# The two down projections read their tokens in another order

## The chip, the cores and the metric

The kernel runs on one core of one Trainium2 chip. The metric is the device time of one execution in microseconds (us). TensorE multiplies, VectorE (DVE), ScalarE (ACT) and GpSimd (POOL) work on the elements beside it, and the SP queue issues the loads of the weights. On-chip operands lie in SBUF, sums of TensorE in the eight banks ps0 to ps7 of PSUM.

## The reference, cut to what matters

256 tokens of width 2048 pass two transformer blocks. Each block ends with a feed-forward part, whose last product is the down projection and a residual sum:

```
x = x + (silu(h @ w_gate) * (h @ w_up)) @ w_down            # block 1, hidden width 5632
h = h + (silu(conv(gate)) * conv(val)) @ w_down_2           # block 2, hidden width 5632
```

The sum over the hidden width is made for each token by itself: the order in which the tokens are gone through changes nothing in the result, as long as each sum is added to its own token.

## The kernel before, in words

Everything is held transposed: features on the 128 partitions, the 256 tokens (T) along the free dimension. X is the residual stream, 16 tiles of 128 features x 256 tokens in float32. HID holds the hidden activations of a feed-forward part: 44 tiles (FT) of 128 features x 256 tokens, each in two parts, a high part rounded to the reduced format fp32r and a low part with what is left.

The weights pass through as "units". A unit is 2048 columns: two row tiles of 128 x 1024, brought by the SP queue with two loads of 512 KB into one of four slots of RAW. ACT writes its rounded copy to HIW (line 606, two slots), DVE writes the difference to LOW (line 1073, in the slot of RAW), and TensorE uses both. For each of the unit's two row tiles and each of eight blocks of 128 output columns, `unit` issues three matmuls, high weight times high activation (L1947), high times low (L1948) and low times high (L1949). So a unit is 2 x 8 x 3 = 48 matmuls. The stationary operand is the 128 x 128 block of weights; the moving operand is the activation tile, 256 columns of 4 bytes that lie one behind the other; the output goes to columns 0 to 255 of bank f. A large part of the program (input, output, gate and up projections) does this with H_ROWS as the moving operand; the down projections do it with HID.

A down projection (`down` in each engine's program) is two halves of 1024 output features. Each half is 22 units over the 44 tiles of HID and sums into the eight banks; then `residual` on DVE (L1650) adds the eight banks to eight tiles of X, one instruction of 128 x 256 for each bank, and frees the bank with `bank_freed`. TensorE's first matmul into a bank of the next half waits for that. The first down projection is followed by the projections of the attention, the second by 32 transposes of X (L2454), copies to OUTT and the stores of the output.

The order between engines is kept by semaphores alone: ACT waits until TensorE is through with the unit two before (`unit_used`), DVE for ACT (`hi_made`), TensorE for DVE (`lo_made`).

Of the kernel before, what the change touches and what calls it, by code (L numbers as in the profile page):

```python
# [20 lines left out]
ALU = mybir.AluOpType  # L21
# [4 lines left out]
T = 256  # L26
# [59 lines left out]
def build(nc, io, out):  # L86
    with ExitStack() as ctx:
# [6 lines left out]
        def S(name):  # L94
            if name in after:
                name = after[name][0]
            if name not in sems:
                sems[name] = ctx.enter_context(nc.semaphore(name))
            return sems[name]
# [21 lines left out]
        def at(name, shape, offset, dt=F32):  # L121
            return nc.alloc_sbuf_tensor_at(name, shape, dt, offset=offset)
# [10 lines left out]
        X = at("X", [P, KT, T], o); o += 16384  # L133
# [111 lines left out]
        HID = at("HID", [P, 2, FT, T], r2, F32R)  # L245
# [31 lines left out]
        ps = [ctx.enter_context(nc.psum_tensor(f"ps{i}", [P, 512], F32)) for i in range(8)]  # L277
# [10 lines left out]
        U_DOWN1 = U_FFN1 + 11 * UG  # L288
# [4 lines left out]
        U_DOWN2 = U_FFN2 + 11 * UG  # L293
# [5 lines left out]
        N_DOWN1 = N_FFN1 + 88  # L299
# [3 lines left out]
        N_DOWN2 = N_FFN2 + 88  # L303
# [3 lines left out]
        M_IN, M_OUT, M_FFN1, M_DOWN1, M_FOX, M_OUT2, M_FFN2, M_DOWN2 = 2, 44, 58, 135, 149, 191, 205, 282  # L307
# [4 lines left out]
        bank_freed = S("bank_freed")  # L312
# [747 lines left out]
        def _(dve):  # L1060
            V = nc.vector
# [7 lines left out]
            def lo(u_const, g=None, stepu=0):  # L1069
                v = u_const + 1  # L1070
                dve.wait_ge(hi_made, v if g is None else g * stepu + v)
                n = unit_cols(u_const)
                V.tensor_tensor(LOW[:, u_const % 4, 0:n], RAW[:, u_const % 4, 0:n],  # L1073
                                HIW[:, u_const % 2, 0:n].bitcast(F32), ALU.subtract).then_inc(lo_made, 1)

            def summed(n7, f, u_end, g=None, nf=8, stepu=UG):
                if f < nf - 1:
                    v = n7 + f + 1
                    dve.wait_ge(tile_summed, v if g is None else g * 7 + v)
                else:  # L1080
                    v = u_end + FREE_UNITS
                    dve.wait_ge(unit_used, v if g is None else g * stepu + v)
# [24 lines left out]
            def h_low(k, fs):  # L1107

                c = COL[GAIN[k]]
                for f in fs:  # L1110
                    dve.wait_ge(S("h_hi"), KT * k + f + 1)
                    V.scalar_tensor_tensor(H(1, f, f + 1)[:, 0, :], X[:, f, :], vec[:, c + f:c + f + 1],  # L1112
                                           H(0, f, f + 1)[:, 0, :].bitcast(F32), ALU.mult, ALU.subtract)\
                        .then_inc(S("h_made"), 1)
# [18 lines left out]
            for i, pack in list(enumerate(PACKS))[1:]:  # L1133
                r = sum(n for _, n in pack)
                b = 3 + (i - 1) % 5
# [507 lines left out]
            o_low(3).then_inc(S("mix_made"), 1)  # L1643


            def residual(m0, u_end, half):
                for f in range(GROUP):
                    summed(m0, f, u_end)
                    x = X[:, half * 8 + f, :]
                    V.tensor_tensor(x, x, ps[f][:, 0:T], ALU.add).then_inc(bank_freed, 1)  # L1650

            def out_phase(u0, m0, k):
                for j in range(2, UG + 1):
                    lo(u0 + j)
                residual(m0, u0 + UG, 0)
                lo(u0 + UG + 1)
                u = u0 + UG
                for j in range(2, UG + 1):
                    lo(u + j)
                    if j < 6:  # L1660
                        h_low(k, (2 * j - 4, 2 * j - 3))
                residual(m0 + 7, u + UG, 1)
                lo(u + UG + 1)
                h_low(k, range(8, KT))

            def down(u0, m0, last=False):
                b = u0
                with dve.Fori(0, 4) as i:
                    for j in range(4):
                        lo(b + 6 + j, i, 4)  # L1670
                lo(b + 22)
                residual(m0, b + 22, 0)
                lo(b + 23)
                b = u0 + FT // 2
                for j in range(4):
                    if not last and j < 2:
                        h_low(2, range(4 * j, 4 * j + 4))
                    lo(b + 2 + j)
                with dve.Fori(0, 4) as i:
                    for j in range(4):  # L1680
                        lo(b + 6 + j, i, 4)
                if not last:
                    lo(b + 22)
                residual(m0 + 7, b + 22, 1)
                if not last:
                    lo(b + 23)
                    h_low(2, range(8, KT))
# [5 lines left out]
            def ffn_phase(u0, evac, tail, k, eps):  # L1693
                for j in range(2, UG):
                    lo(u0 + j)
                    if j == 6:
                        variance(k, eps)
                    elif j == 7:
                        inverse_root(k)
                with dve.Fori(0, 10) as g:  # L1700
                    lo(u0 + UG, g, UG)
                    evac(g)
                    for j in range(1, UG):
                        lo(u0 + UG + j, g, UG)
                        tail(g, j)
                lo(u0 + 11 * UG)
                evac(10)
                for j in range(1, UG):
                    if j < 6:
                        lo(u0 + 11 * UG + j)  # L1710
                    tail(10, j)
# [14 lines left out]
                                    HID[:, 0, bass.ds(g * 4, 4), :].bitcast(F32), ALU.subtract)\  # L1726
                        .then_inc(S("hid_made"), 1)
            ffn_phase(U_FFN1, evac_ffn1, tail_ffn1, 1, 1e-5)
            down(U_DOWN1, M_DOWN1)

            def evac_fox(g):
                for f in range(GROUP):
# [167 lines left out]
                                    HID[:, 0, bass.ds(g * 4, 4), :].bitcast(F32), ALU.subtract)\  # L1900
                        .then_inc(S("hid_made"), 1)
            ffn_phase(U_FFN2, evac_ffn2, tail_ffn2, 3, 1e-6)
            down(U_DOWN2, M_DOWN2, last=True)
            for q in range(4):
                got("turned_v")
                V.tensor_copy(OUTT[:, 1, q * 512:(q + 1) * 512], ps[4 + q][:, :]).then_inc(S("y_tokens_1"), 1)
# [3 lines left out]
        def _(pe):  # L1910
# [50 lines left out]
            def group_phase(u0, n0, groups, wcol=plain, h_wait={}):  # L1961
                with pe.Fori(0, groups) as g:
                    for j in range(UG):
                        unit(u0 + j, [2 * j, 2 * j + 1], GROUP, wcol, j == 0, j == UG - 1, g, UG, n0, h_wait=h_wait.get(j))
# [13 lines left out]
                    if j == 4:  # L1978
                        square_sums_out(k, pairs)

            def down(u0, n0, made0):

                for half in range(2):
                    b = u0 + half * (FT // 2)
                    for j in range(2):
                        unit(b + j, [2 * j, 2 * j + 1], GROUP, plain, j == 0, n0=n0 + 8 * half,
                             hcol=lambda part, k: HID[:, part, k, :], h_wait=(S("hid_made"), made0 + 10))
                    with pe.Fori(0, 4) as i:
                        for j in range(4):
                            unit(b + 2 + j, [4 + 2 * j, 5 + 2 * j], GROUP, plain, g=i, step=4,  # L1990
                                 hcol=lambda part, k: HID[:, part, bass.ds(i * 8 + k, 1), :])
                    for j in range(18, 22):
                        unit(b + j, [2 * j, 2 * j + 1], GROUP, plain, last=j == 21,
                             hcol=lambda part, k: HID[:, part, k, :], h_wait=(S("hid_made"), made0 + 11))

            pe.sem_inc(unit_used, FREE_UNITS)
            pe.wait_ge(S("ident_made"), 1)
            for n in range(NT):
# [5 lines left out]
                for q in range(4):  # L2004
                    for i in range(4):
                        f = 4 * q + i
# [4 lines left out]
            for j in range(4):  # L2011
                if j == 3:
                    pe.wait_ge(S("vecs_landed"), counts["vecs_landed"])
                    for i, pack in list(enumerate(PACKS))[1:]:
                        r = sum(n for _, n in pack)
                        b = 3 + (i - 1) % 5
                        if i <= 5 and b > 3:
                            pe.wait_ge(S("x_second"), b - 3)
                        if i > 5:
                            pe.wait_ge(S("vecs_made"), i - 4)  # L2020
                        nc.tensor.transpose(ps[b][:, (i // 6) * P:(i // 6) * P + r], VPACK[0:r, i, :],
                                            ident[0:r, 0:r]).then_inc(S("vecs_turned"), 1)
                unit(j, [4 * j + i for i in range(4)], 3, lambda kk, f: kk * 384 + f * P, j == 0, j == 3,
                     n0=N_MISC1, h_wait=0)
# [89 lines left out]
            for fill, kind in enumerate(FILLS):  # L2114
# [4 lines left out]
                dst, i = ps[fill % 8], place[kind]  # L2119
# [58 lines left out]
            for c in range(NCH):  # L2178
                cc = slice(c * C, c * C + C)
                s0 = ST[:, c % 2]  # L2180
                for hb in range(2):
                    if c:
                        got("s_out")
                    for i in range(4):
                        t = 4 * hb + i
# [17 lines left out]
                for hb in range(2):  # L2203
# [3 lines left out]
                    for i in range(4):  # L2207
                        t = 4 * hb + i
# [4 lines left out]
                for hb in range(2):  # L2213
# [3 lines left out]
                    for i in range(4):  # L2217
                        t = 4 * hb + i
# [29 lines left out]
            for lev in range(1, 6):  # L2248
# [15 lines left out]
                for c in range(NCH):  # L2264
                    got("inv_pm")
                    b = INV_BANKS[c]
# [98 lines left out]
            group_phase(U_OUT, N_OUT, 2, h_wait={0: (S("mix_made"), 1), 4: (S("mix_made"), 2)})  # L2365
            first_group(U_FFN1, N_FFN1, 1, ((SUM_BANK, NSQ[:, 0, :]),), gate_up_col)
            group_phase(U_FFN1 + UG, N_FFN1 + 8, 10, gate_up_col)
            down(U_DOWN1, N_DOWN1, 1)

            def sum_squares(g):  # L2370
                pe.wait_ge(S("sq_lo"), g)
# [73 lines left out]
            group_phase(U_OUT2, N_OUT2, 2)  # L2445
            first_group(U_FFN2, N_FFN2, 3, ((SUM_BANK, NSQ[:, 0, :]),), gate_up_col)
            group_phase(U_FFN2 + UG, N_FFN2 + 8, 10, gate_up_col)
            down(U_DOWN2, N_DOWN2, 12)

            pe.wait_ge(bank_freed, N_END + FREE_BANKS)  # L2450
            for n in range(NT):
# [21 lines left out]
```

## Time and profile before

| what | value |
|---|---|
| median of 3 runs | 2509.73 us (2506.45 to 2510.35) |
| profiled execution, its own time | 2507.64 us |
| its span | 2505.9 us |
| TensorE busy | 2439.3 us, 97% of the span |
| DVE / ACT / POOL busy | 1484.8 / 1122.4 / 114.1 us |
| mean granted clock of TensorE | 0.992 of full speed |
| read from HBM | 427.59 MB |

The span is what the profile covers; the execution's own time is 1.74 us longer. Matmuls are pipelined: the durations of single ones overlap, so their pace is read from the distance between starts, not from the durations.

### The profile page before, as it was taken

To read this page: it belongs to the slowest core of one execution; us is meant where nothing else is said; L and a number is where in the kernel's file an instruction comes from. 1 tells how busy PE (TensorE), PEld (TensorE's weight loads), DVE (VectorE), ACT (ScalarE), POOL (GpSimd) and SP (SyncE) were. 2 spreads that over 40 slices of the span, in tenths; PEclk is the share of its full clock that TensorE was granted. 3 is DMA by queue.
4 is the path that set the end of the run, shared out by engine and by line. 5 is a ranking of instruction groups with operands and counts; after the bars stand their busy time and mean duration, and the time that the engine had idled before them with its cause. 6 is when DMAs were issued, how large, how long until landed. Compare 5 with 4: busy or idle time off the path is not lost.

```text
span 2505.9 us, 57361 instructions
## 1 busy us (share of the span) xinstructions
PE 2439.3 (97%) x24650; PEld 2411.0 (96%) x24650; DVE 1484.8 (59%) x1683; ACT 1122.4 (45%) x1061; POOL 114.1 (5%) x93
## 2 busy tenths in 40 slices
PE   7999978989999999999999999999999999999998
PEld 7999968889999999999999999989999999999998
DVE  6557597665555555554444567674576666665444
ACT  4334424354444444443344443454455555544332
POOL 3000050000200000000020200000200000000000
PEclk9999989999999999999999999999999999999999
DMA  7455400116555555556665565625555555555554
GB/s 232 166 187 196 135 6 4 37 69 193 188 190 197 188 195 190 193 192 192 194 192 194 169 237 200 218 86 191 187 194 191 194 189 196 187 197 188 200 187 148
DMA packets 171387, 431.72 MB, mean 172 GB/s; under 512 B 17614, under 2 KB 23387, under 8 KB 170107
## 3 DMA queue, kind: packets, MB, share of 16 engines
q1 hardware_dynamic: 170027, 422.30, 50.0%
q10 hardware_dynamic: 1232, 7.52, 0.8%
q8 instruction: 104, 1.70, 0.3%
q14 instruction: 24, 0.20, 0.0%
HBM read 427.59 MB, written 2.17 MB: 171 GB/s over the span
## 4 chain that ended last, share of the span: by engine, by line
PE 91%; DVE 7%; ACT 2%; issue 1%; DMA 0%; DVEq 0%; SPq 0%; ACTq 0%
PE ps L1947 28%; PE ps L1948 28%; PE ps L1949 28%; DVE LOW L1073 1%; ACT HIW L606 1%; PE ps L2101 1%; DVE TM L1346 0%; ACT H_ROWS L648 0%; DVE LO L1350 0%; DVE TT L1347 0%; DVE CV L1380 0%; DVE GT L1362 0%; PE ps L2139 0%; DVE TMP L1293 0%; PE ps L2045 0%
## 5 line engine op out<-in xcount | busy, mean ns | idle before, releaser
L1073 DVE TENSOR_TENSOR LOW<-RAW,HIW 128x2048 fp32r<-128x2048 f32 (+1 forms) x397 | 911.9, 2297 | 921.9 <-ACT HIW L606 921.8
L1947 PE MATMUL ps<-H_ROWS,HIW 128*128 128x256 f32 x4928 | 1367.3, 277 | 20.1 <-DVE LOW L1073 17.5
L1948 PE MATMUL ps<-H_ROWS,HIW 128*128 128x256 f32 x4928 | 1366.1, 277 | 0.0
L1949 PE MATMUL ps<-H_ROWS,LOW 128*128 128x256 f32 x4928 | 1364.9, 277 | 0.0
L606 ACT ACTIVATE HIW<-RAW 128x2048 fp32r<-128x2048 f32 (+1 forms) x397 | 760.8, 1917 | 1196.4 <-PE ps L1949 1192.5
L1947 PEld LDWEIGHTS ps<-H_ROWS,HIW 128*128 128x128 f32 x4928 | 928.4, 188 | 22.1 <-DVE LOW L1073 18.5
L1949 PEld LDWEIGHTS ps<-H_ROWS,LOW 128*128 128x128 f32 x4928 | 928.9, 188 | 0.0
L1948 PEld LDWEIGHTS ps<-H_ROWS,HIW 128*128 128x128 f32 x4928 | 928.1, 188 | 0.1
L1947 PE MATMUL ps<-HID,HIW 128*128 (+1 forms) x1408 | 388.7, 276 | 0.0
L1948 PE MATMUL ps<-HID,HIW 128*128 (+1 forms) x1408 | 388.6, 276 | 0.0
L1949 PE MATMUL ps<-HID,LOW 128*128 (+1 forms) x1408 | 388.6, 276 | 0.0
L1947 PEld LDWEIGHTS ps<-HID,HIW 128*128 128x128 f32 x1408 | 264.3, 188 | 0.2 <-issue 0.2
L1949 PEld LDWEIGHTS ps<-HID,LOW 128*128 128x128 f32 x1408 | 264.3, 188 | 0.0
L1948 PEld LDWEIGHTS ps<-HID,HIW 128*128 128x128 f32 x1408 | 264.3, 188 | 0.0
L528 POOL TENSOR_TENSOR NSQ<-NSQ 128x1024 f32<-128x1024 f32 (+2 forms) x12 | 30.0, 2498 | 500.1 <-ACT NSQ L634 499.5
L1891 DVE SCALAR_TENSOR_TENSOR YG<-UC,vec,YG 128x256 f32<-128x256 f32 x88 | 42.1, 478 | 0.0
L1891 DVE SCALAR_TENSOR_TENSOR YV<-UC,vec,YV 128x256 f32<-128x256 f32 x88 | 42.0, 478 | 0.0
L528 POOL TENSOR_TENSOR SQA<-SQA 128x1024 f32<-128x1024 f32 (+1 forms) x4 | 9.8, 2460 | 605.5 <-ACT SQA L640 605.3
L1117 DVE TENSOR_TENSOR UC<-ps,rstd 128x256 f32<-128x256 f32 x88 | 30.1, 412 | 0.0
L648 ACT ACTIVATE H_ROWS<-X,vec 128x256 fp32r<-128x256 f32 x64 | 27.0, 494 | 0.0
L1112 DVE SCALAR_TENSOR_TENSOR H_ROWS<-X,vec,H_ROWS 128x256 fp32r<-128x256 f32 x64 | 26.7, 478 | 0.0
L1042 ACT ACTIVATE YV<-UC,vec 128x256 f32<-128x256 f32 x44 | 25.9, 588 | 0.0
(365 smaller groups left out, 1515.3 us busy)
## 6 DMA issues: line engine op xcount, KB each, us to landing
RAW<-in_ffn_w_up SPq DMA_DIRECT2D x264, 512.0 KB, 4.3
RAW<-in_ffn_w_down SPq DMA_DIRECT2D x176, 512.0 KB, 4.5
RAW<-in_fox_w_in SPq DMA_DIRECT2D x98, 512.0 KB, 4.4
RAW<-in_w_in SPq DMA_DIRECT2D x96, 512.0 KB, 4.1
RAW<-in_ffn_w_gate SPq DMA_DIRECT2D x88, 512.0 KB, 3.7
RAW<-in_w_out SPq DMA_DIRECT2D x32, 512.0 KB, 5.0
RAW<-in_fox_w_out SPq DMA_DIRECT2D x32, 512.0 KB, 4.8
INV<-rows_out ACTq DMA_DIRECT2D x4, 1024.0 KB, 7.5
```

The source lines that it names most:

```text
L528: tick(nc.gpsimd.tensor_tensor(sq[:, 0:n, :], sq[:, 0:n, :], sq[:, n:2 * n, :], ALU.add), "pool_step")
L606: A(HIW[:, u_const % 2, 0:n], RAW[:, u_const % 4, 0:n], ACT.Copy).then_inc(hi_made, 1)
L648: A(H(0, f, f + 1)[:, 0, :], X[:, f, :], ACT.Copy, scale=vec[:, c + f:c + f + 1]).then_inc(S("h_hi"), 1)
L1042: ins = A(conv_out(i), UC[:, i, 0:T], ACT.Identity, scale=conv_tap(g, 0, i), bias=vec[:, bass.ds(g * 4 + (cb + (i % 2) * FT + i // 2), 1)])
L1073: V.tensor_tensor(LOW[:, u_const % 4, 0:n], RAW[:, u_const % 4, 0:n], HIW[:, u_const % 2, 0:n].bitcast(F32), ALU.subtract).then_inc(lo_mad ...
L1112: V.scalar_tensor_tensor(H(1, f, f + 1)[:, 0, :], X[:, f, :], vec[:, c + f:c + f + 1], H(0, f, f + 1)[:, 0, :].bitcast(F32), ALU.mult, ALU ...
L1117: return V.tensor_tensor(dst, ps[f][:, 0:T], rstd[:], ALU.mult)
L1891: ins = V.scalar_tensor_tensor(conv_out(i), UC[:, i, j - 1:j - 1 + T], conv_tap(g, j - 1, i), conv_out(i), ALU.mult, ALU.add)
L1947: mm(o_, hi_w, h_hi, start=start, stop=False)
L1948: mm(o_, hi_w, h_lo, start=False, stop=False)
L1949: i = mm(o_, lo_w, h_hi, start=False, stop=stop)
L2101: ins = mm(dst[rr, i * P:(i + 1) * P], src[rr, t, cc], AR[rr, t, :, cc], start=True, stop=True)
```

## The change

The moving operand of every matmul of a down projection is read through another access pattern. In the first down projection ("odd last") the 256 tokens of a tile are read as 0, 2, 4, ..., 254, 1, 3, ..., 255: two runs of 128 with a step of 8 bytes. In the second ("halves") they are read as 0, 128, 1, 129, ..., 127, 255: pairs whose two members lie 512 bytes apart. The sums stand in the banks in the order in which the tokens were read. `residual` reads the bank in that order and reads and writes X through the same pattern as the matmuls used, so that X stays in the order of the tokens. The number of instructions, their sizes, the weights, the layout of HID and X and all waits are the same.

```diff
+            def ordered(x, order):
+                if order == "odd last":
+                    return x.rearrange("p (i e) -> p e i", e=2)
+                return x.rearrange("p (e i) -> p i e", e=2)
...
-                    x = X[:, half * 8 + f, :]
-                    V.tensor_tensor(x, x, ps[f][:, 0:T], ALU.add).then_inc(bank_freed, 1)
+                    x, y = X[:, half * 8 + f, :], ps[f][:, 0:T]
+                    if order is not None:
+                        x = ordered(x, order)
+                        y = y.rearrange("p (e i) -> p e i", e=x.shape[1])
+                    V.tensor_tensor(x, x, y, ALU.add).then_inc(bank_freed, 1)
...
-            down(U_DOWN1, M_DOWN1)
+            down(U_DOWN1, M_DOWN1, "odd last")
-            down(U_DOWN2, M_DOWN2, last=True)
+            down(U_DOWN2, M_DOWN2, "halves", last=True)
...
             # TensorE, in the three places of down
-                             hcol=lambda part, k: HID[:, part, k, :], h_wait=(S("hid_made"), made0 + 10))
+                             hcol=lambda part, k: ordered(HID[:, part, k, :], order), h_wait=(S("hid_made"), made0 + 10))
-                                 hcol=lambda part, k: HID[:, part, bass.ds(i * 8 + k, 1), :])
+                                 hcol=lambda part, k: ordered(HID[:, part, bass.ds(i * 8 + k, 1), :].rearrange("p k t -> p (k t)"), order))
...
-            down(U_DOWN1, N_DOWN1, 1)
+            down(U_DOWN1, N_DOWN1, 1, "odd last")
-            down(U_DOWN2, N_DOWN2, 12)
+            down(U_DOWN2, N_DOWN2, 12, "halves")
```

## Rows read from the trace of the kernel before

**Rows 1.** The page: busy time, TensorE's granted clock by slice, and the chain that ended last

```profile
PE 2439.3 (97%) x24650; PEld 2411.0 (96%) x24650; DVE 1484.8 (59%) x1683; ACT 1122.4 (45%) x1061; POOL 114.1 (5%) x93
...
PEclk9999989999999999999999999999999999999999
...
PE 91%; DVE 7%; ACT 2%; issue 1%; DMA 0%; DVEq 0%; SPq 0%; ACTq 0%
```

**Rows 2.** Groups of instructions: the matmuls of the down projections

```profile
L1947 PE MATMUL ps<-HID,HIW 128*128 (+1 forms) x1408 | 388.7, 276 | 0.0
L1948 PE MATMUL ps<-HID,HIW 128*128 (+1 forms) x1408 | 388.6, 276 | 0.0
L1949 PE MATMUL ps<-HID,LOW 128*128 (+1 forms) x1408 | 388.6, 276 | 0.0
L1947 PEld LDWEIGHTS ps<-HID,HIW 128*128 128x128 f32 x1408 | 264.3, 188 | 0.2 <-issue 0.2
```

**Rows 3.** Matmuls on HID, busy time by stretch (from:to, length, PE busy, clock, DMA share, GB/s)

```profile
1120.00:1370.00 250.00, 239.53 (x2112) 1.00 0.60 193
2250.00:2500.00 250.00, 239.82 (x2112) 1.00 0.53 179
```

**Rows 4.** Timeline of PE, first and last matmul of each down projection (start, length)

```profile
1127.23 0.28 PE L1947 MATMUL ps<-HID,HIW 128*128 128x256 f32 x1
...
1366.48 0.28 PE L1949 MATMUL ps<-HID,LOW 128*128 128x256 f32 x1
...
2255.93 0.28 PE L1947 MATMUL ps<-HID,HIW 128*128 128x256 f32 x1
...
2495.48 0.28 PE L1949 MATMUL ps<-HID,LOW 128*128 128x256 f32 x1
```

**Rows 5.** Timeline of DVE and ACT around the middle of the second down projection

```profile
2367.18 2.29 DVE L1073 TENSOR_TENSOR LOW<-RAW,HIW 128x2048 fp32r<-128x2048 f32 x1 [3.15 <-ACT HIW L606]
2372.68 2.29 DVE L1073 TENSOR_TENSOR LOW<-RAW,HIW 128x2048 fp32r<-128x2048 f32 x1 [3.21 <-ACT HIW L606]
2374.89 2.73 DVE L1650 TENSOR_TENSOR X<-X,ps 128x256 f32<-128x256 f32 x8
2378.12 2.29 DVE L1073 TENSOR_TENSOR LOW<-RAW,HIW 128x2048 fp32r<-128x2048 f32 x1 [0.50 <-ACT HIW L606]
...
2370.73 1.92 ACT L606 ACTIVATE HIW<-RAW 128x2048 fp32r<-128x2048 f32 x1 [3.58 <-PE ps L1949]
```

**Rows 6.** Groups of ACT and DVE that read elements one behind the other

```profile
L606 ACT ACTIVATE HIW<-RAW 128x2048 fp32r<-128x2048 f32 (+1 forms) x397 | 760.8, 1917 | 1196.4 <-PE ps L1949 1192.5 <-DMA RAW<-in_fox_w_in 3.5 <-DMA RAW<-in_w_in 0.3
...
L634 ACT ACTIVATE NSQ<-X 128x1024 f32<-128x1024 f32 x8 | 8.0, 1045 | 0.0
...
L1459 DVE COPY UU<-ps 128x256 f32<-128x256 f32 x8 | 3.4, 425 | 8.4 <-PE ps L2210 8.2
...
L1121 DVE COPY vec<-ps 128x16 f32<-128x16 f32 x1 | 0.2, 174 | 10.3 <-PE ps L2002 10.3
```

**Rows 7.** Groups of DVE whose read steps 256 bytes from element to element

```profile
L1594 DVE COPY small<-QG 128x16 f32<-128x16 f32 x2 | 0.3, 172 | 1.4 <-ACT QG L879 1.4
...
L1306 DVE COPY small<-EG 128x32 f32<-128x32 f32 x1 | 0.2, 193 | 0.0
```

**Rows 8.** Line 2075, whose moving operand steps 8 bytes in runs of four

```profile
L2075 PE MATMUL ps<-ident,ROWS x16: 209/209/231, 336.7 to 337.2; 128*64 128x16 f32 x16
```

**Rows 9.** Timeline of the end, and the residual sums of the second down projection

```profile
2493.41 2.80 DVE L1650 TENSOR_TENSOR X<-X,ps 128x256 f32<-128x256 f32 x8 [4.25 <-PE ps L1949]
...
2496.27 3.71 PE L2454 MATMUL ps<-ident,X 128*128 128x128 f32 x32 [0.51 <-DVE X L1650]
...
L1650 DVE TENSOR_TENSOR X<-X,ps x16: 409/417/422, 2374.9 to 2495.8; 128x256 f32<-128x256 f32 x16
```

More of the change, by code:

```diff
@@ L1643, in _, with residual @@
             o_low(3).then_inc(S("mix_made"), 1)
-            def residual(m0, u_end, half):
+            def ordered(x, order):
+                if order == "odd last":
+                    return x.rearrange("p (i e) -> p e i", e=2)
+                return x.rearrange("p (e i) -> p i e", e=2)
+            def residual(m0, u_end, half, order=None):
                 for f in range(GROUP):
                     summed(m0, f, u_end)
-                    x = X[:, half * 8 + f, :]
-                    V.tensor_tensor(x, x, ps[f][:, 0:T], ALU.add).then_inc(bank_freed, 1)
+                    x, y = X[:, half * 8 + f, :], ps[f][:, 0:T]
[3 more added lines that the diff above has]
+                    V.tensor_tensor(x, x, y, ALU.add).then_inc(bank_freed, 1)
             def out_phase(u0, m0, k):
@@ L1664, in out_phase, with down @@
                 h_low(k, range(8, KT))
-            def down(u0, m0, last=False):
+            def down(u0, m0, order, last=False):
                 b = u0
@@ L1671, in down @@
                 lo(b + 22)
-                residual(m0, b + 22, 0)
+                residual(m0, b + 22, 0, order)
                 lo(b + 23)
@@ L1683, in down @@
                     lo(b + 22)
-                residual(m0 + 7, b + 22, 1)
+                residual(m0 + 7, b + 22, 1, order)
                 if not last:
@@ L1979, in first_group, with ordered, down @@
                         square_sums_out(k, pairs)
-            def down(u0, n0, made0):
+            def ordered(h, order):
+                if order == "odd last":
+                    return h.rearrange("p (i e) -> p e i", e=2)
+                return h.rearrange("p (e i) -> p i e", e=2)
+            def down(u0, n0, made0, order):
                 for half in range(2):
@@ L1990, in down @@
                             unit(b + 2 + j, [4 + 2 * j, 5 + 2 * j], GROUP, plain, g=i, step=4,
-                                 hcol=lambda part, k: HID[:, part, bass.ds(i * 8 + k, 1), :])
+                                 hcol=lambda part, k: ordered(HID[:, part, bass.ds(i * 8 + k, 1), :].rearrange("p k t -> p (k t)"), order))
                     for j in range(18, 22):
                         unit(b + j, [2 * j, 2 * j + 1], GROUP, plain, last=j == 21,
-                             hcol=lambda part, k: HID[:, part, k, :], h_wait=(S("hid_made"), made0 + 11))
+                             hcol=lambda part, k: ordered(HID[:, part, k, :], order), h_wait=(S("hid_made"), made0 + 11))
             pe.sem_inc(unit_used, FREE_UNITS)
```

## The prediction

> **What bounds the kernel now.** I began with the page. TensorE is busy 97% of the span, its clock stands at the full 2.4 GHz level in nearly every slice, and the chain that ended last is 91% TensorE [rows 1]. That only says that TensorE is worth a look, since overlapping matmuls look busy at any pace. So I went on to the matmuls that the change touches: 3 groups of 1408 on HID, with no idle time ahead of them [rows 2]. That makes 4224, and the stretches show 2112 in each down projection at a granted clock of 1.00 [rows 3]. The pace comes from the first and last start. In the first projection 1366.48 - 1127.23 = 239.25 us for 2111 steps is 113.3 ns a matmul; in the second 2495.48 - 2255.93 = 239.55 us is 113.5 ns [rows 4]. 256 columns at 2.4 GHz, one a cycle, are 106.7 ns. So the stream of the moving operand fills all but 6.7 ns of each step, and its pace is the pace of the stage.
>
> Then I asked what else could set the stage. In a down projection DVE makes one LOW per unit, 5.44 us apart (2378.12 - 2372.68), which is 48 matmuls of 113.3 ns; it works 2.29 us of that and waits for ACT, and ACT works 1.92 us and waits 3.58 us for TensorE [rows 5]. Everybody waits for TensorE. The loads hold the DMA engines 0.53 to 0.60 of the time [rows 3]. The two down projections are 478.8 us, 19% of the span, bound by how fast TensorE takes its columns.
>
> **The change, part by part.** No instruction is added or removed, and no wait is. The outputs in PSUM stay contiguous. Three things are moved: the moving reads of 2112 matmuls to steps of 8 bytes, those of 2112 others to pairs 512 bytes apart, and the X side of 32 residual sums to the same patterns.
>
> *The matmuls, second projection (halves).* No row shows TensorE reading a long moving operand in another order, so I bound it. From below: 0, if the array is fed one column a cycle whatever the addresses. From above I take DVE's copies with a step of 256 bytes: 16 elements take 172 ns and 32 take 193 ns, so 21 / 16 = 1.3 ns an element [rows 7], against (425 - 174) / 240 = 1.05 ns for elements in a row [rows 6]. So SBUF gives scattered elements at least once in 1.3 ns. For 256 columns that is 333 ns, 219.7 ns more than 113.3, and times 2112 it is +464 us. Between these ends I count in whole cycles of the array: one cycle a column costs nothing, two are 0.83 ns a column and three 1.25 ns, which is the upper bound in another dress. I take two cycles. The trace's readers point there: ACT takes (1917 - 1045) / 1024 = 0.85 ns an element in a row, DVE 1.05 ns [rows 6]; TensorE takes one in 0.42 ns. No other reader takes 4-byte elements faster than one in 0.85 ns, and TensorE's rate is twice that. I read it as more than one element won from one access, which works for neighbours and not for tokens 128 apart. At one element an access TensorE falls to about ACT's rate, the two-cycle case. DVE, which needs only one in 1.05 ns, shows little of it, and that is what rows 7 have.
>
> The price: the stream grows from 106.7 to 213.3 ns. If the 6.7 ns on top are paid again the step is 220 ns and the stage grows by 106.7 x 2112 = 225.3 us; if they are hidden behind the longer stream (the weight load beside it is 188 ns long in its row [rows 2]), by (213.3 - 113.3) x 2112 = 211.2 us. I take the middle, +218.3 us. Nothing hides it, for TensorE is the bound. A unit then lasts some 10.4 us, so ACT, DVE and the loads have only more room.
>
> The Trainium skill speaks against this change: "SBUF — State Buffer", section "Door 1: The DMA port swizzle", says that SBUF has lines of 16 bytes and that an access pattern needs at least two hits on a line for full bandwidth, each crossing to a new line being paid. By it the pairs 512 bytes apart have one hit a line and are slow, and the 8-byte steps have two and are free; it gives no figure for the penalty, and the sum by it is the one taken here. No row here shows it either way for TensorE, and DVE's copies [rows 7] show almost none.
>
> *The matmuls, first projection (odd last).* Bounds are the same, 0 and +464 us. I take 0: an 8-byte step still leaves each element a near neighbour to share an access with. The nearest row is line 2075, a moving operand in 8-byte steps: 16 columns in 209 ns [rows 8], with no stall that could be seen. It is weak evidence, as 16 columns are few and the product is plain float32.
>
> *The residual sums.* DVE starts one every 0.34 us, paced by TensorE (eight in 2.73 us), though each lasts 0.41 us [rows 5, 9]. With X in steps, the price by rows 7 is (1.3 - 1.05) x 256 = 64 ns each; the bounds are 0 and a doubled element time, 267 ns. In the middle of a projection and after the first one this is hidden: a bank is wanted again 8 x 0.34 = 2.7 us after its last matmul, and the lateness at the eighth bank would be 8 x 0.267 = 2.1 us at worst. If the cover were gone it would cost what exceeds 2.7 us. Behind the sums on DVE stand one LOW, which has 3 us to spare [rows 5], and after the first projection the low parts of H. At the end of the kernel they are on the path: the transposes wait for the eighth sum [rows 9]. There halves costs 0.06 us if TensorE's own pace has slowed to 0.65 us a bank, since DVE then keeps up, and 8 x 0.064 = 0.5 us (2.1 us at worst) if it hasn't. I take 0.1 us.
>
> *The sum.* 2507.64 (the profiled execution's own time, 1.74 over its span) + 218.3 + 0 + 0.1 = 2726.0 us. That execution lies 2.1 us under the median of the runs, so in the terms of the runs it is 2728 us, 8.7% more than before.
>
> **The rivals.**
>
> *Nothing happens (the other side: not slower).* The reader of the moving operand keeps up in any order. One mechanism: it delivers a scattered column within 113.3 / 256 = 0.44 ns, by fetching ahead or because two fetched places stay open, between which the pairs alternate. For it speaks that each 512-byte pair walks along two runs in order, and that DVE's copies at 256 bytes lose nearly nothing [rows 7]; against it, that no row shows a scattered element in less than 1.3 ns. It decides from that 0.44 ns on: at 0.5 ns a column the stage is already 31 us longer. The time would be 2510 us, at most 2 us more from the last residual sums.
>
> *Both orders are slow.* If only direct neighbours share an access, steps of 8 bytes have none. Then the first projection pays the same: +436.6 us, 2946 us. Against it stands rows 8, weakly.
>
> *Halves costs three cycles a column.* If each access in another place is as slow for TensorE as DVE's 1.3 ns [rows 7], the step is 320 to 333 ns, and the second projection alone gives 2112 x 207 to 220 ns = +437 to +464 us, 2947 to 2974 us. Against it: DVE's element takes 1.05 ns without any step, so its 1.3 ns is mostly DVE's own.
>
> *A part of it.* The fetches overlap and only some columns stall: +5 to +100 us, 2515 to 2610 us.
>
> **How the numbers follow.** Forecast 0.55, nothing 0.24, both slow 0.10, three cycles 0.05, a part 0.04, and 0.02 for a gain that I have no mechanism for. The predicted time is the first case's, 2728 us; its own range is 2712 to 2745, from the two prices of the step and the spread of the runs, and a little above for a step that is not whole cycles. The cases over 2900 hold 0.15. A range that takes in all the others reaches from 2505 to 2760 and holds some 0.8. Slower by over 0.2% (5 us, about what a measurement of this kernel can tell from no change) is 0.55 + 0.10 + 0.05 + 0.04 = 0.74, within it 0.24, faster 0.02.
>
> **What would show it.** In the profile of the changed kernel: starts of the matmuls on HID 113 ns apart in the first projection and 213 to 220 ns apart in the second, a stretch of 239 us and one of some 458 us; single durations up from 276 to about 383 ns; LOW every 10.4 us instead of 5.44 us with DVE and ACT waiting longer; the clock still 1.00, or, if it fell to the 1.2 GHz level, no loss beyond this, as that level takes one column in 0.83 ns too. The residual sums would be 0.41 to 0.48 us. The prediction is wrong if the second projection keeps 113 ns, if the first one's step moves, or if the step of the second isn't near two cycles a column.

## The result: 2755 us, and the loss stands in the other projection

| | before | changed |
|---|---|---|
| median of 4 runs | 2509.17 us (2506.45 to 2510.35) | 2755.46 us (2754.96 to 2755.75) |
| span of the profiled execution | 2505.9 us | 2754.0 us |

The ratio is 1.098 (95% interval 1.0967 to 1.0994). The loss of 246 us lies near the forecast of 218 us, but it isn't where the forecast put it. The page of the changed kernel says so in its slices (the mean busy share of DVE and the rates of the loads, 68.9 us a slice):

```profile
PE 2686.7 (98%) x24650; PEld 2613.1 (95%) x24650; DVE 1487.2 (54%) x1683; ACT 1121.7 (41%) x1061; POOL 110.2 (4%) x93
...
DVE  6557677755555545312221246767457666676444
PEclk9999999999999999999999999999999999999999
...
GB/s 211 179 188 197 62 4 19 79 153 184 198 187 194 194 188 197 137 92 97 102 92 91 98 129 186 246 199 138 154 185 197 191 190 198 187 195 193 196 193 152
```

TensorE is as busy as before. The loads fall to half, 91 to 102 GB/s, in slices 18 to 23, which is 1170 to 1580 us: the first down projection. In the last slices, where the second one runs, they are what they were. The stretches of the matmuls on HID give the size (two of 100 us in each projection; columns as in [rows 3]; a stretch also counts the one to three matmuls that reach into it):

```profile
1140.00:1240.00 100.00, 100.00 (x438) 1.00 0.31 95
1400.00:1500.00 100.00, 100.00 (x438) 1.00 0.30 95
2510.00:2610.00 100.00, 99.86 (x895) 1.00 0.61 193
2630.00:2730.00 100.00, 100.00 (x898) 1.00 0.60 189
```

438 matmuls in 100 us in the first projection, 898 in the second, at the full clock in both. Steps are better read from the timeline, first to last start:

```profile
1129.17 0.39 PE L1956 MATMUL ps<-HID,HIW 128*128 128x256 f32 x1
...
1613.28 0.41 PE L1958 MATMUL ps<-HID,LOW 128*128 128x256 f32 x1
...
2505.49 0.27 PE L1956 MATMUL ps<-HID,HIW 128*128 128x256 f32 x1
...
2742.39 0.28 PE L1958 MATMUL ps<-HID,LOW 128*128 128x256 f32 x1
```

The first projection takes 1613.28 - 1129.17 = 484.11 us; over 2111 steps that is 229.3 ns a matmul with steps of 8 bytes, against 113.3 before [rows 4]. The second takes 2742.39 - 2505.49 = 236.90 us, 112.2 ns with the pairs 512 bytes apart, against 113.5. So the order of which I expected nothing costs 244.9 us, and the order that was to cost 218 us costs nothing and gives 2.6 us back.

DVE shows the reverse (the residual sums of the first and of the second projection):

```profile
L1659 DVE TENSOR_TENSOR X<-X,ps x16: 421/422/423, 1366.7 to 1613.7; 128x256 f32<-128x256 f32 x16
```

```profile
L1659 DVE TENSOR_TENSOR X<-X,ps x16: 583/621/633, 2622.9 to 2743.6; 128x256 f32<-128x256 f32 x16
...
2741.29 2.90 DVE L1659 TENSOR_TENSOR X<-X,ps 128x256 f32<-128x256 f32 x6
2744.24 0.98 PE L2469 MATMUL ps<-ident,X 128*128 128x128 f32 x7 [1.57 <-DVE X L1659]
```

With 8-byte steps on X they are as long as in order, with pairs 512 bytes apart they go from 0.417 us [rows 9] to 0.621 us. At the end that is on the path: from the last matmul's start to the first transpose it is 2744.24 - 2742.39 = 1.85 us, against 2496.27 - 2495.48 = 0.79 us [rows 4, 9]. The rest of the 248.1 us between the two spans (244.9 - 2.6 + 1.1 = 243.4) is 4.7 us in stretches whose reads the change leaves alone, 1.9 us ahead of the first projection and 2.8 us between the two. The runs of before lie 3.9 us apart, so this may be chance; nothing here shows a cause for it.

### The profile page after: what moved, and what is told of

Read it like the earlier page. It is cut to its first block, busy times and chain, and to the rows that moved or that the text cites. A ratio compares the mean times of both kernels' runs of the same rounds, so it can differ in the third digit from the quotient of the medians.

```text
span 2754.0 us, 57361 instructions
## 1 busy us (share of the span) xinstructions
PE 2686.7 (98%) x24650; PEld 2613.1 (95%) x24650; DVE 1487.2 (54%) x1683; ACT 1121.7 (41%) x1061; POOL 110.2 (4%) x93
## 4 chain that ended last, share of the span: by engine, by line
PE 92%; DVE 6%; ACT 2%; issue 0%; DMA 0%; DVEq 0%; SPq 0%; ACTq 0%
PE ps L1956 29%; PE ps L1957 28%; PE ps L1958 28%; DVE LOW L1073 1%; ACT HIW L606 1%; PE ps L2116 1%; PE ps L2107 0%; DVE TM L1346 0%; ACT H_ROWS L648 0%; DVE LO L1350 0%; DVE TT L1347 0%; DVE CV L1380 0%; DVE GT L1362 0%; PE ps L2060 0%; PE ps L2154 0%
## 5 line engine op out<-in xcount | busy, mean ns | idle before, releaser
L1956 PE MATMUL ps<-HID,HIW 128*128 (+1 forms) x1408 | 482.5, 343 | 0.1
L1958 PE MATMUL ps<-HID,LOW 128*128 (+1 forms) x1408 | 481.8, 342 | 0.0
L1957 PE MATMUL ps<-HID,HIW 128*128 (+1 forms) x1408 | 481.8, 342 | 0.0
L1956 PEld LDWEIGHTS ps<-HID,HIW 128*128 128x128 f32 x1408 | 281.8, 200 | 15.6 <-issue 0.3
L1958 PEld LDWEIGHTS ps<-HID,LOW 128*128 128x128 f32 x1408 | 281.9, 200 | 14.9
L1957 PEld LDWEIGHTS ps<-HID,HIW 128*128 128x128 f32 x1408 | 281.8, 200 | 14.9
L1659 DVE TENSOR_TENSOR X<-X,ps 128x256 f32<-128x256 f32 x64 | 25.4, 465 | 11.7 <-PE ps L1958 11.7
```

The costliest lines, as they stand in the source:

```text
L1659: V.tensor_tensor(x, x, y, ALU.add).then_inc(bank_freed, 1)
L1956: mm(o_, hi_w, h_hi, start=start, stop=False)
L1957: mm(o_, hi_w, h_lo, start=False, stop=False)
L1958: i = mm(o_, lo_w, h_hi, start=False, stop=stop)
```

## The experiments

In all of them `ordered` takes another pattern, and each half of a down projection can have its own (1056 matmuls, of which the first and the last start give the step). DVE's `residual` takes the same pattern over X where all 256 tokens are read by steps or by `swap`; elsewhere it adds the bank in plain order, so that e4, e5, e6 and e8 add some sums to other tokens or leave tokens out, and only their times are read. e2 was executed 12 times and e7 5 times, each of the others once; the step of an order comes back to 0.1 ns in other executions (229.3 ns in the changed kernel and in e1). With `h` one tile of HID, 256 tokens of 4 bytes, the patterns in short:

```diff
+ ("step", n):   h.rearrange("p (i e) -> p e i", e=n)              # 2: odd last; 128: halves
+ ("swap", n):   h.rearrange("p (g e i) -> p g i e", e=2, i=n)     # 2: 0,2,1,3, 4,6,5,7, ...
+ ("turns", e, i): the same with e runs of i in turn
+ "third":       h[:, 0:252].rearrange("p (i e) -> p e i", e=3)
+ ("pairs", o):  h[:, o:o+252].rearrange("p (i e j) -> p e i j", e=2, j=2)
+ ("runs", j, o, n): h[:, o:o+n].rearrange("p (i e j) -> p e i j", e=2, j=j)
+ "six of eight": h.rearrange("p (i j) -> p i j", j=8)[:, :, 0:6]
+ ("cut", n):    h.rearrange("p (i e) -> p e i", e=2)[:, :, 0:n]    # 2n columns
+ ("first", n):  h[:, 0:n]
```

**e1, the two orders change places.**

```diff
-            down(U_DOWN1, N_DOWN1, 1, "odd last")
+            down(U_DOWN1, N_DOWN1, 1, (("step", 128), ("step", 128)))
...
-            down(U_DOWN2, N_DOWN2, 12, "halves")
+            down(U_DOWN2, N_DOWN2, 12, (("step", 2), ("step", 2)))
```

> The two orders change places: pairs 512 bytes apart (halves) in the first down projection, steps of 8 bytes (odd last) in the second. If the cost belongs to the order, the first keeps a step of 112 to 113 ns a matmul and the second goes to 230 ns, and the whole is again some 2754 us. If it belongs to the place (something in the first projection that doubles its step whatever the order), the first stays at 230 ns and the second at 112 ns. The residual sums with 8-byte steps stay at 0.42 us, those with 512-byte pairs at 0.62 us, wherever they stand.

2750.82 us. Stretches of the matmuls on HID, two in each projection:

```profile
1130.00:1230.00 100.00, 100.00 (x898) 1.00 0.64 197
1250.00:1350.00 100.00, 100.00 (x898) 1.00 0.63 192
2300.00:2400.00 100.00, 100.00 (x437) 1.00 0.31 96
2500.00:2600.00 100.00, 100.00 (x438) 1.00 0.31 98
```

By starts: 111.7 and 112.4 ns in the halves of the first projection, 229.3 and 229.3 ns in the second. The cost goes with the order, not with the place. The residual sums went along too (0.632 us in the first).

**e2, pairs 512 bytes apart in both projections.** The edit is `("step", 128)` in all four places.

> Pairs 512 bytes apart in both down projections, 8-byte steps nowhere. If the whole loss came from the 8-byte steps, the time is that of the kernel before: the profile after shows a step of 112.2 ns for this order against 113.4 ns before, so 4224 matmuls would give back 5 us, and the slower residual sums at the end cost 1.1 us: 2505 us, a ratio of 0.998. If the shorter step is chance, the ratio is 1.000. If the pairs cost what I had predicted, only not in the second projection, it would be 2728 us.

2505.22 us against 2512.09 us of the kernel before on the same chip, a ratio of 0.9971 (0.9959 to 0.9982). The whole loss was the 8-byte steps. By starts the first projection takes 236.5 us here and 484.1 us in the changed kernel, 247.6 us for 2112 matmuls; the two medians, taken on different chips, differ by 2755.46 - 2505.22 = 250.2 us. The small gain is clear of the noise, since the interval ends below 1.

**e3, other steps.** First projection ("step", 4) and ("step", 8), second ("step", 64) and ("step", 32).

> Other steps between columns, one for each half of a projection: 4 elements (16 bytes) and 8 elements (32 bytes) in the first, 64 elements (four runs in turn, 256 bytes apart) and 32 elements (eight runs in turn, 128 bytes apart) in the second. Theory A, the moving reader gets two neighbouring words (8 bytes) in one access and a few such pairs stay open: 16 and 32 bytes cost 230 ns as 8 bytes did, not more; 64 elements stays at 113 ns if four pairs can stay open and goes to 230 ns if only two can, 32 elements likewise for eight. Theory B, even and odd words come from two sides of the memory with one word per two cycles each, and a short queue sorts them: 16 and 32 bytes 230 ns; 64 and 32 elements slow as soon as the queue is shorter than the run of equal sides. Theory C, a long innermost run with a step is read at half rate whatever the addresses and a short one isn't: 230 ns for runs of 64 and 32 elements, less for runs of 4 and 8. Theory D, two columns are fetched at a time and clash when they lie in the same bank: some of these steps are free and others slow, with no order from short to long.

2894.86 us. One stretch of 100 us in each half:

```profile
1150.00:1250.00 100.00, 100.00 (x430) 1.00 0.31 95
1400.00:1500.00 100.00, 100.00 (x456) 1.00 0.32 101
2500.00:2600.00 100.00, 100.00 (x700) 1.00 0.48 156
2700.00:2800.00 100.00, 100.00 (x457) 1.00 0.30 95
```

By starts 233.3, 220.0, 143.3 and 220.0 ns. A longer step is hardly dearer than 8 bytes: 233.3 ns is 0.91 ns a column, and 32 bytes are a little cheaper than 8. Some two cycles of 2.4 GHz a column (0.83 ns) is what all of them come to. Four runs in turn cost a quarter more, eight cost the full factor of two. D falls (from 8 to 32 bytes all are slow alike), C doesn't fit the short innermost runs of 8, which are as slow as those of 32. A and B stay.

**e4, the orders that tell A and B apart.** First projection "third" and ("pairs", 1), second ("pairs", 0) and ("swap", 2).

> Four orders that set the theories apart; in three of the halves the sums of 252 columns are of other tokens than before and 4 tokens are left out, and there the residual sum reads the bank in plain order. First projection: steps of 12 bytes (every third token), then pairs of direct neighbours that begin at odd words (1,2, 5,6, ...). Second: the same pairs beginning at even words (0,1, 4,5, ...), then 0,2,1,3, 4,6,5,7, ..., neighbours 8 bytes apart whose pairs are completed at once. Theory A (aligned 8 bytes in one access, some stay open): 226 ns, 226 ns, 112 ns, 113 ns. Theory B (even and odd words from two sides): 112 ns for the 12-byte steps, since even and odd alternate, 112 ns for the odd pairs, 112 ns, 113 ns. Theory C (long stepped run slow): 226 ns for the first, about 112 ns for the other three. Theory D (two columns 8 bytes apart clash): 226 ns or 112 ns for the first, 112 ns for both kinds of pairs, 230 ns for the last.

2870.16 us.

```profile
1150.00:1250.00 100.00, 100.00 (x447) 1.00 0.33 101
1400.00:1500.00 100.00, 100.00 (x443) 1.00 0.32 101
2500.00:2600.00 100.00, 100.00 (x443) 1.00 0.30 95
2740.00:2840.00 100.00, 100.00 (x851) 1.00 0.59 186
```

By starts 224.4, 226.7, 226.6 ns (252 columns) and 117.8 ns (256). All four theories fall. Two neighbours in the same 8 bytes, followed by a gap of two, are as slow as steps of 8 bytes (against A and C), 12-byte steps are slow though even and odd words alternate (against B), and 0,2,1,3 costs only 4.5 ns more than plain order though neighbours lie 8 bytes apart (against D). What the fast orders seem to have in common is that all four words of 16 bytes are used within a few columns; the others leave words out, or come back too late.

**e5, what is the unit?** First projection ("runs", 4, 0, 256) and ("runs", 4, 2, 248), second ("runs", 8, 0, 256) and "six of eight".

> What unit does the reader fetch? Four orders made of runs of neighbours with gaps, one for each half of a projection: runs of 4 that begin at multiples of 16 bytes (0-3, 8-11, ..., then 4-7, 12-15, ...), the same beginning 8 bytes later (2-5, 10-13, ..., 248 columns); then runs of 8 (0-7, 16-23, ...), and six of each eight tokens (0-5, 8-13, ..., 192 columns). Where columns are left out or doubled the sums are of other tokens; the residual sum reads the bank in plain order. Theory E: the memory is read in lines of 16 bytes, full speed needs the whole line used while it is open, and a column costs two cycles, but a line never more than four. It has the pairs of the run before at half speed (two of four words of a line used), two and four runs in turn at or near full speed, and gives here 113 ns for the runs of 4, some 222 ns for the shifted ones (each touches two lines with two hits), 113 ns for the runs of 8, and 4/3 cycles a column, some 120 ns, for six of eight. Theory F, lines of 32 bytes: 229 ns, 222 ns, 113 ns, 120 ns. Theory G, lines of 64 bytes: 229, 222, 229 and 120 ns. If a gap as such costs half the speed, 176 ns for the last.

2635.68 us.

```profile
1130.00:1230.00 100.00, 100.00 (x852) 1.00 0.61 186
1300.00:1400.00 100.00, 100.00 (x453) 1.00 0.30 94
2380.00:2480.00 100.00, 100.00 (x836) 1.00 0.55 181
2510.00:2610.00 100.00, 100.00 (x872) 1.00 0.59 188
```

By starts 117.8, 221.3 (248 columns), 120.0 and 115.0 ns (192 columns). The same runs of four are fast at multiples of 16 bytes and slow 8 bytes later. Of the three theories only E, lines of 16 bytes, has both this and full or nearly full speed for the runs of 8; F had 229 ns for the first half, G for the first and the third. E had 113 ns for the runs of four and of eight, though, and the 4.5 and 6.7 ns that they take beyond it are not accounted for. E's 4/3 cycles for six of eight (120 ns forecast) came out at 115, near the floor that e6 shows, so this half confirms only that it isn't two cycles (176 ns).

**e6, fewer columns.** First projection ("cut", 96) and ("cut", 64), second ("first", 192) and ("first", 128).

> Fewer columns for each matmul, so that part of the tokens' sums is left out; the residual sum stays whole. First projection, steps of 8 bytes: 192 and then 128 columns. Second, in order: 192 and then 128 columns. It tells what stands on top of the two cycles a column: the stepped matmul takes 229.3 ns where 256 x 2 cycles are 213.3. If the rest is a fixed 16 ns a matmul: 176 and 123 ns. If it is in proportion (0.896 ns a column): 172 and 115 ns. For the columns in order: if the stream sets the step of 113.3 ns, 87 and 60 ns; if the weight load beside it does, 113 ns for both. The latter would mean that in the unchanged kernel the stream is hidden behind the weight load and has 6 ns of room.

2571.09 us. Stretches, one in each half:

```profile
1150.00:1250.00 100.00, 100.00 (x579) 1.00 0.40 126
1320.00:1420.00 100.00, 100.00 (x858) 1.00 0.60 189
2330.00:2430.00 100.00, 99.86 (x894) 1.00 0.63 198
2450.00:2550.00 100.00, 100.00 (x898) 1.00 0.59 186
```

Steps of 8 bytes: 173.3 and 116.8 ns by starts. With 229.3 ns for 256 columns that is (229.3 - 173.3) / 64 = 0.875 and (173.3 - 116.8) / 64 = 0.883 ns a column and about 5 ns on top: in proportion, and a little over two cycles (0.833 ns). In order: 112.0 ns for 192 columns (111.7 without its one long step of 0.4 us) and 111.6 ns for 128. Half the columns take the same step. So what bounds the stage is not the stream alone: each matmul with its weight load has a floor of 111.6 ns that doesn't depend on its columns, and 256 columns in order lie only 1.7 ns above it. I had called this floor the weight load beforehand, and that is not shown: every matmul of these kernels has a load, and no run changes its size. The trace of the kernel before has one place that makes it doubtful. 64 matmuls on SQH and SQL have a stationary operand of 16 columns instead of 128 and the same 256 moving columns in order; their loads take 94 ns in their rows instead of 188 [rows 2], and yet they start 116.7 ns apart:

```profile
L2376 PEld LDWEIGHTS ps<-SQH,sel1r x32: 93/94/94, 1463.8 to 1602.0; 128*16 128x16 f32 x32
```

**e7, pairs 512 bytes apart in all projections,** and the banks read back in token order (the copy to PR, which isn't shown, and the residual sums get the same pattern as `scaled`):

```diff
 def h_in(part, k):
-                return H(part, k, k + 1)[:, 0, :]
+                return H(part, k, k + 1)[:, 0, :].rearrange("p (e i) -> p i e", e=2)
 def scaled(dst, f):                                   # the evacuation; residual and the copy to PR alike
-                return V.tensor_tensor(dst, ps[f][:, 0:T], rstd[:], ALU.mult)
+                return V.tensor_tensor(dst.rearrange("p (e i) -> p e i", e=2),
+                                       ps[f][:, 0:T].rearrange("p (i e) -> p e i", e=2),
+                                       rstd[:].rearrange("p (e i) -> p e i", e=2), ALU.mult)
```

> The pairs 512 bytes apart in every matmul of the projections, also the 14784 that read H_ROWS; the banks are read back with steps of 8 bytes in PSUM and X, rstd and the targets in token order. The two down projections alone gave a ratio of 0.9971, with a step of 112.1 to 112.4 ns against 113.3. If the gain belongs to the order, 1 ns on 19008 matmuls is 19 us less, a ratio of 0.993. If it belongs to HID's place in memory or is chance, the ratio stays at 0.997 to 1.000. If DVE's reads of PSUM with steps are much slower than 0.41 us, the evacuations hold up TensorE at the ends of groups, and the time goes above the kernel before.

2472.69 us against 2511.89 us on the same chip: a ratio of 0.9831 (0.981 to 0.9852), faster than the kernel before by twice what I had expected. A stretch of 500 us in the second block's gate and up projections, before and with e7:

```profile
1700.00:2200.00 500.00, 498.92 (x4380) 498.67 (x4379) 322.51 (x360) 262.48 (x222) 15.73 (x7) 1.00 0.56 192
```

```profile
1700.00:2200.00 500.00, 498.76 (x4465) 498.52 (x4464) 335.45 (x386) 271.88 (x234) 15.58 (x7) 1.00 0.60 195
...
L1675 DVE TENSOR_TENSOR X<-X,ps x16: 410/415/422, 2341.9 to 2461.0; 128x256 f32<-128x256 f32 x16
2461.48 3.71 PE L2503 MATMUL ps<-ident,X 128*128 128x128 f32 x32 [0.51 <-DVE X L1675]
```

4465 matmuls against 4380, 112.0 ns a step against 114.2, with some 1.6 us of waits in each. The starts one by one, over all 19008 matmuls, show two parts of the gain. Most steps in plain order are 113 or 114 ns, 113.3 in the mean, and become 111.7. And 1277 of them take 116 ns or more: in most groups 24 to 26 in a row, in the group's last unit, at 119 ns. In e7 two are left. So 1.7 ns on each of 19008 is 32 us and the long ones are 7 us, together the 39 us between the medians. What makes the long ones is open. The evacuation of the banks by DVE, which comes next to them, doesn't fit: a row of them starts at 1037.02 us in the kernel before and ends at 1040.12, while DVE reads the banks from 1038.66 to 1041.39.

```profile
1036.91 0.28 PE L1949 MATMUL ps<-H_ROWS,LOW 128*128 128x256 f32 x1
1037.02 0.28 PE L1947 MATMUL ps<-H_ROWS,HIW 128*128 128x256 f32 x1
1037.14 0.28 PE L1948 MATMUL ps<-H_ROWS,HIW 128*128 128x256 f32 x1
1037.26 0.28 PE L1949 MATMUL ps<-H_ROWS,LOW 128*128 128x256 f32 x1
...
1038.66 0.42 DVE L1117 TENSOR_TENSOR SG<-ps,rstd 128x256 f32<-128x256 f32 x1
```

The residual sums are back at 0.415 us: DVE can step through a bank by 8 bytes and over X in order for nothing, where the pairs on X cost 0.2 us each. That also takes away small waits in the middle of the down projections: in e7 their four halves run at 111.7, 111.7, 112.1 and 111.7 ns, while with the slow sums (e2) the second halves stood at 112.4.

**e8, runs in turn that lie close together.** First projection ("turns", 2, 4) and ("turns", 2, 16), second ("turns", 4, 4) and ("turns", 8, 4).

> Runs read in turn, now close together; all tokens are summed and the residual sum reads the bank in plain order, so that the sums go to other tokens. First projection: two runs 16 bytes apart (0,4,1,5,2,6,3,7, 8,12, ...) and two runs 64 bytes apart (0,16,1,17, ...). Second: four runs 16 bytes apart (0,4,8,12,1,5, ...) and eight (0,4,...,28,1,5, ...). What is known: two runs 512 bytes apart take 112.1 ns, four runs 256 bytes apart 143.3 ns, eight runs 128 bytes apart 220.0 ns, neighbours in the order 0,2,1,3 117.8 ns. If it is the number of 16-byte lines that must stay open (two are, four hardly, eight are not), the distance is nothing: 112, 112, 143 and 220 ns. If the lines clash by their place in memory (256 and 128 bytes being the same place), the near runs are faster than the far ones: some 113 ns for four, and less than 220 ns for eight. If the gain of 1.2 ns over the plain order comes from taking two lines in turn, both orders of two show 112 ns and not 113.3.

2665.30 us.

```profile
1140.00:1240.00 100.00, 100.00 (x898) 1.00 0.64 195
1260.00:1360.00 100.00, 100.00 (x898) 1.00 0.64 199
2280.00:2380.00 100.00, 100.00 (x738) 1.00 0.50 163
2450.00:2550.00 100.00, 100.00 (x418) 1.00 0.28 90
```

By starts 111.7, 111.7, 136.0 and 240.0 ns, beside 112.1 (512 bytes apart), 143.3 (256) and 220.0 (128). It is the number of lines in turn that counts. The distance changes 5 to 9%, and not in one direction: four near runs are faster than four far ones, eight near ones slower, so a clash by place in memory is not what makes eight slow.

All orders together:

| columns read | words used of each 16 bytes, lines in turn | ns a matmul |
|---|---|---|
| in order | 4, one | 113.3 |
| two runs in turn, 16, 64 or 512 bytes apart | 4, two | 111.7 to 112.4 |
| 0,2,1,3, 4,6,5,7 | 4, one | 117.8 |
| runs of 4 or 8 on 16-byte places, with gaps | 4, one | 117.8, 120.0 |
| four runs in turn | 4, four | 136.0, 143.3 |
| eight runs in turn | 4, eight | 220.0, 240.0 |
| pairs with gaps, at even or odd words | 2 | 226.6, 226.7 (252 columns) |
| runs of 4, shifted by 8 bytes | 2 | 221.3 (248 columns) |
| steps of 8, 12, 16, 32 bytes | 2, 1 or 2, 1, 1 | 229.3, 224.4 (252 columns), 233.3, 220.0 |

## Why the time was forecast right, and the reason wrong

The total was right by luck. It came within 28 us of the number, and 4.5 us under the upper end of the wide range (2505 to 2760 us), because one of the two orders costs about two cycles a column, as priced, and each is used by 2112 matmuls. It was the other one. The forecast's own range of 2712 to 2745 us doesn't hold 2755, and all three signs that the prediction gave for being wrong came true: the second projection kept its step, which so isn't near two cycles a column, and the first one's moved. Step by step:

*What bounds the kernel* was half right. Everybody waits for TensorE, as said. But "the stream of the moving operand fills all but 6.7 ns of each step, and its pace is the pace of the stage" was wrong as a reading: 128 columns take 111.6 ns as well (e6). The step has two nearly equal bounds, the stream and a floor for each matmul with its weight load. I had named the load only as something beside the stream [rows 2], and never asked what a matmul with fewer columns would take. It didn't spoil the sum, since the slow stream is far above both.

*The matmuls, second projection (halves)*, +218.3 us, is a step that failed. Measured -2.6 us. I reasoned that what lets TensorE take a word in 0.42 ns is "more than one element won from one access, which works for neighbours and not for tokens 128 apart". The first part holds, and the conclusion doesn't: e5 shows the 16 bytes as the unit, and two such lines can be read in turn at full speed (e1, e2, e8). The simplest reading is that both stay usable while the columns alternate, so each line still gives all its four words; if each column fetched its line anew, these orders would be as slow as steps of 16 bytes. My rival "nothing happens" had named that mechanism, "because two fetched places stay open", with a chance of 0.24. For this projection the runs bear it out.

*The matmuls, first projection (odd last)*, 0 taken, is the other step that failed, and the larger one: 244.9 us. I took it that an 8-byte step "still leaves each element a near neighbour to share an access with". It does, but one neighbour isn't enough: two words of four used is half speed (e4, e5). The rival "both orders are slow" (0.10) had this projection's cost in it, but for another reason: it let direct neighbours share an access, and direct neighbours with a gap behind them are slow too (e4). The upper bound of 464 us held. The line that I leaned on, 2075 with 16 columns in 209 ns [rows 8], could not have shown it. 16 columns at 0.42 ns more are 7 ns.

*The size.* For two cycles a column I had 220 ns or 213.3 ns a matmul; measured are 229.3 ns. e6 shows where it lies for this order: 0.88 ns a column and not 0.833, which is 12 ns on 256 columns. The term was 26.6 us short (244.9 against 218.3). Why it is more than two whole cycles is open, the more so as the orders of 32-byte steps and of eight runs at 128 bytes take 220.0 ns, the number forecast.

*The residual sums.* The pairs cost 0.2 us each, not 0.064; the bound of 0.267 held. The 0.064 was a poor reading: it set three short copies out of SBUF in steps [rows 7] against copies out of PSUM in order [rows 6]. At the end that is 1.06 us where I took 0.1. In the middle they were nearly hidden: the half that follows runs at 112.4 ns where e7, with quick sums, has 111.7, which is 0.7 ns x 1055 = 0.7 us. The 8-byte steps on X cost nothing.

Of the Trainium skill's rule, two hits on a 16-byte line for full bandwidth ("SBUF — State Buffer", section "Door 1: The DMA port swizzle"), the runs bear out the 16-byte line and not the two hits, for TensorE's 4-byte moving operand: two hits are half speed, four are full speed (e4, e5). Nor is each crossing paid, as two lines in turn are the fastest order of all. DVE's sums over X fit the two hits: 0.422 us with 8-byte steps, and in e3, with 16 and 32 bytes, 0.637 to 0.692 us:

```profile
L1672 DVE TENSOR_TENSOR X<-X,ps x16: 637/645/692, 1370.9 to 1608.2; 128x256 f32<-128x256 f32 x16
```

## What to carry to other kernels

Read a 4-byte moving operand of TensorE (fp32r here, the only format tried) so that each aligned 16 bytes is used whole within a few columns. A jump to a second run is free, the order 0,2,1,3 within the 16 bytes costs 4%, and a step of two words already costs the full factor of two. If an order has to be undone, undo it where DVE reads PSUM, not by scattering its SBUF operand. And when an instruction could be paced by two things of nearly the same length, as here the stream (an estimate of 106.7 ns for 256 columns, one a cycle) and a floor of 111.6 ns for each matmul, the profile's durations don't tell which it is; changing the size of one does.

## What the runs showed that I had not expected

Two runs in turn are faster than plain order, 111.7 against 113.3 ns, and the rows of steps at 119 ns go away too; that is 1.7% of the whole kernel (e7). Shown are the gain and that it goes with two lines in turn at 16, 64 and 512 bytes (e8). 111.7 ns is the floor that e6 shows, so the stream no longer adds to the step. Why the plain order stays 1.7 ns above the floor is open; that the reader gets more time for each line when it holds two is an argument and wasn't tried by itself. Open too is how the reader treats partly used lines: steps of 16 bytes touch twice as many lines as steps of 8 and take the same time (233.3 and 229.3 ns), so it isn't the number of lines fetched that sets the two cycles.
